# Tile 0's last quarter of features ahead of the last product, and a gate's copy between tile 1's halves, at the end of the second layer's output projection

## What is computed

```python
y = jnp.concatenate([y_sc, y_mla, y_cf, y_na], axis=-1) @ p["w_out"]
x = x + ga1 * rmsnorm(y, p["g_post_mix"])
hm = rmsnorm(x, p["g_pre_mlp"]) * (1 + sc2) + sh2
x = x + ga2 * rmsnorm(sq_relu_mlp(hm, p["w_mlp1"], p["w_mlp2"]), p["g_post_mlp"])
```

## Time and profile before

| | |
|---|---|
| median of three runs | 1489.4 us (1488.3 to 1489.86) |
| the profiled execution's own time | 1490.7 us |
| its span | 1488.8 us |
| TensorE (PE) busy | 1439.2 us, 97% |
| VectorE (DVE) busy | 908.9 us, 61% |
| ScalarE (ACT) busy | 671.6 us, 45% |
| the tail of this change, about | 827 to 851 us of the span |

### The profile page before, as it was taken

The page is one execution under the profiler, slowest core; times in us unless marked ns, Lnnn a source line. Parts: engine busy times, 40 slices in busy tenths (PEclk is TensorE's granted clock), DMA queues, the critical chain, the costliest instruction groups (busy, mean ns, idle before and its releaser), DMA issues.

```text
span 1488.8 us, 23403 instructions
## 1 busy us (share of the span) xinstructions
PE 1439.2 (97%) x9394; PEld 1231.1 (83%) x9394; DVE 908.9 (61%) x1388; ACT 671.6 (45%) x1060; POOL 38.0 (3%) x55
## 2 busy tenths in 40 slices
PE   5999998999999999999999999999999999999998
PEld 3787655888888888889856888998999999798996
DVE  3776555563241433579755665568998545796867
ACT  4421355562140413465155844455444564664544
POOL 0000000000000000000060000000000000000000
PEclk9999999999999999999999999999999999999999
DMA  9421675041331314236375555465445434455553
GB/s 394 160 85 57 236 290 211 4 159 65 114 112 59 132 35 144 82 126 218 114 269 212 198 189 178 147 221 184 170 170 170 165 133 145 142 195 192 176 198 114
DMA packets 33562, 236.95 MB, mean 159 GB/s; under 512 B 3712, under 2 KB 3840, under 8 KB 5696
## 3 DMA queue, kind: packets, MB, share of 16 engines
q1 hardware_dynamic: 32080, 228.31, 42.3%
q0 software_dynamic: 1392, 7.34, 1.5%
HBM read 234.58 MB, written 1.05 MB: 158 GB/s over the span
## 4 chain that ended last, share of the span: by engine, by line
PE 85%; DVE 5%; ACT 4%; DMA 4%; issue 1%; SPq 0%; DVEq 0%; ACTq 0%
PE ps L551 44%; PE ps L597 23%; PE ps L571 4%; DMA w<-in_stream 3%; PE ps L760 2%; PE ps L653 1%; PE ps L840 1%; PE ps L956 1%; DVE w_lo L436 1%; DMA U<-in_start 1%; PE ps L989 1%; PE ps L973 1%; ACT w_hi L426 1%; PE ps L961 1%; PE ps L689 1%
## 5 line engine op out<-in xcount | busy, mean ns | idle before, releaser
L551 PE MATMUL ps<-h_hi,w_hi 128*128 128x256 f32 (+1 forms) x1504 | 468.6, 312 | 3.7 <-DVE h_lo L2487 0.9
L551 PE MATMUL ps<-h_hi,w_lo 128*128 128x256 f32 (+1 forms) x1504 | 464.7, 309 | 0.0
L551 PE MATMUL ps<-h_lo,w_hi 128*128 128x256 f32 (+1 forms) x1504 | 464.6, 309 | 0.0
L426 ACT ACTIVATE w_hi<-w 128x1024 fp32r<-128x1024 f32 x332 | 333.2, 1053 | 246.3 <-DMA w<-in_stream 246.2
L436 DVE TENSOR_TENSOR w_lo<-w,w_hi 128x1024 fp32r<-128x1024 f32 x332 | 390.7, 1219 | 82.1 <-ACT w_hi L426 77.4
L551 PEld LDWEIGHTS ps<-h_hi,w_hi 128*128 128x128 f32 x1504 | 287.0, 191 | 20.6 <-issue 3.2
L551 PEld LDWEIGHTS ps<-h_lo,w_hi 128*128 128x128 f32 x1504 | 287.1, 191 | 15.0 <-issue 0.5
L551 PEld LDWEIGHTS ps<-h_hi,w_lo 128*128 128x128 f32 x1504 | 287.0, 191 | 14.5
L597 PE MATMUL ps<-w_hi,g_hi 128*128 128x512 f32 x472 | 185.0, 392 | 1.7 <-DVE g_lo L2340 0.9
L597 PE MATMUL ps<-w_lo,g_hi 128*128 128x512 f32 x472 | 183.8, 389 | 0.0
L597 PE MATMUL ps<-w_hi,g_lo 128*128 128x512 f32 x472 | 183.8, 389 | 0.0
(11 more groups left out here) (291 smaller groups left out, 1749.6 us busy)
## 6 DMA issues: line engine op xcount, KB each, us to landing
w<-in_stream SPq DMA_DIRECT2D x206, 1024.0 KB, 4.9
U<-in_start SPq DMA_DIRECT2D x4, 1024.0 KB, 11.4
w<-in_start SPq DMA_DIRECT2D x2, 1024.0 KB, 10.8
GA<-in_start SPq DMA_DIRECT2D x2, 1024.0 KB, 14.2
U<-in_bias POOLq DMA_DIRECT2D x2, 1024.0 KB, 6.0
SW<-in_small POOLq DMA_DIRECT2D x2, 896.0 KB, 5.0
X<-in_x SPq DMA_DIRECT2D x1, 1024.0 KB, 5.0
X<-in_ctx SPq DMA_DIRECT2D x1, 1024.0 KB, 7.2
```

Source lines behind the costliest of these rows:

```text
L426: act.activation(k.w_hi[:, c.slot, half], k.w[:, c.slot, half], ACT.Copy).then_inc(k.hi_done, 1)
L551: last = pe.matmul(k.banks(2 * c.pair, n, j * (512 if tiles == 2 else n)), w[a][:, c.slot, at:at + 128], h[b][:, kt * stride:kt * stride + n],
```

## The change

On VectorE, part 3 of tile 0's features (one cast, one subtraction) is done right behind part 2, ahead of `product(1, 1)`, instead of behind `residual(1)`. On ScalarE, the copy of the second half gate stands between parts 0, 1 and parts 2, 3 of tile 1's features, instead of ahead of part 0. Nothing is added or removed, and TensorE's, GpSimd's and SyncE's orders are the same.

```diff
@@ act_tail
     if f.to in ("mlp1", "ffn"):
         turn(0)
-    if f.to == "mlp1":
-        act_mod_step(k, act, LAST_GATES[1], 3)
     if f.row is not None:
         row_features(1)
+    elif f.to == "mlp1":
+        features(1, (0, 1))
+        act_mod_step(k, act, LAST_GATES[1], 3)
+        features(1, (2, 3))
     elif f.to:
         features(f.tiles - 1, range(HF_PARTS))
@@ dve_tail
         elif f.to == "mlp1" and t:
-            features(0, (2,))
+            features(0, (2, 3))
         elif f.to and t:
             features(t - 1, (0,))
         product(t, 1)
@@ dve_tail
         elif f.to:
-            if t:
-                features(t - 1, (3,) if f.to == "mlp1" else (2, 3))
+            if t and f.to != "mlp1":
+                features(t - 1, (2, 3))
             norm(t)
```

## The result

Over 22 runs of each, taken in turn, the changed kernel's median is 1493.49 us (1491.20 to 1495.39) and the kernel before's 1490.34 us (1488.30 to 1496.71). The ratio is 1.0015, interval [1.0008, 1.0021]: +2.2 us, between 1.2 and 3.1. It is slower, by less than the 0.2% that the prediction took as its bound (the interval ends at 0.21%), yet clear of no change, and its median lies above the range that was given.

The account below looks back on a forecast made before the run. TensorE, busy for 97% of the span, was taken as the bound, so only its idle stretches counted. Chain +0.61 and copy +0.43 gave +1.0 us on the median 1489.4: 1490.4 us, range 1488.7 to 1492.0.

Parts of the forecast that it names:

- The moved pair lengthens tile 1's chain: VectorE's moved cast and subtraction delay tile 1's residual, scaling and transposes; its first products start +0.61 us late, range 0.45 to 0.70.
- the other tail: Another tail of the same make: transposes 0.63 us after scaling, features 0.66 later; full clock despite a 1.19 us idle stretch.
- The time that the moved pair takes on VectorE: Cast and subtraction ahead of the product: 0.70 us from the trace, chosen over the skill's 0.90.
- The copy between the halves: ScalarE's copy delays parts 2 and 3, so TensorE waits amid tile 1's 24 products: +0.43 us, ends 0.3 and 0.53.
- The stall ahead of the restart moves with the rest: TensorE's 0.77 us wait for ScalarE's reading L1678, ahead of 850.50, stays and shifts with the chain to 851.5.
- TensorE's clock falls: Rival, chance 0.04: new idle stretches drop TensorE to 1.2 GHz for tile 1's 24 products, +4.0 us in all, 1493.4 us.
- one with a fall: Earlier TensorE wait of 2.3 us for a transfer, at 785 us; a 5 us stretch there shows mean clock 0.84.
- the sum: Chain +0.61 and copy +0.43 give +1.0 us on the whole time, ends +0.75 and +1.25; forecast chance 0.62.
- a fall for half of them: Half clock for half of tile 1's 24 products: +2.5 us, still within 0.2%.
- The copy is hidden: Rival, chance 0.20: no wait amid tile 1's products, only the first term stays, +0.6, 1490.0 us.
- The shift is absorbed: Rival, chance 0.07: a later wait that does not follow TensorE ends last, so the end stays, 1489.4 us.
- the gain is kept: Rival, chance 0.05: tile 1's chain has 0.7 us of room, so the first stall's 0.74 + 0.09 us come off, 1488.6 us.

Follow-up runs that it names:

- e1: Against the kernel before: only VectorE's part of the change, ScalarE's order put back. Ratio 0.9999 [0.9991, 1.0008].
- e4: Kernel before plus one unused cast and subtraction on VectorE ahead of the last product, nothing moved. Ratio 1.0001 [0.9992, 1.0010].
- e2: Kernel before with only ScalarE's part of the change, VectorE's order as before. Ratio 1.0004 [0.9994, 1.0014].
- e7: Whole change plus unused matmuls of 512 and 256 columns ahead of tile 1's transposes and products; against the kernel before, ratio 1.0006 [0.9997, 1.0015].
- e3: Whole change plus one unused 512-column float32 matmul behind the second gate; against the kernel before, ratio 1.0000 [0.9991, 1.0009].
- e8: Kernel before with only ScalarE's sine moved ahead of the second turn. Ratio 0.9993 [0.9984, 1.0002].
- e10: Kernel before with ScalarE's sine moved ahead of the second turn, a second time. Ratio 0.9994 [0.9980, 1.0007].
- e6: Whole change plus one unused cast and subtraction on VectorE ahead of the last product; against the kernel before, ratio 1.0023 [1.0014, 1.0032].
- e11: Kernel before with only the gate's copy moved, behind all of tile 1's features. Ratio 0.9995 [0.9984, 1.0007].
- e5: The whole change, unaltered, once more against the kernel before. Ratio 1.0016 [1.0004, 1.0028].
- e9: VectorE's part of the change alone, a second time, against the kernel before. Ratio 1.0003 [0.9991, 1.0015].
- e12: The whole change, unaltered, a third time against the kernel before. Ratio 1.0000 [0.9989, 1.0012].

## Why the prediction was wrong, point by point

**The moved pair lengthens tile 1's chain: right.** Forecast +0.61, measured +0.53 in the change and alone in e1. Part by part: the product was +0.66 late (forecast 0.70), and the transposes began 0.54 us after the scaling (forecast 0.63, from the other tail), the features 0.70 after them (0.66). With the 0.54, the room that tile 1's chain had before was 838.30 - (837.62 + 0.54) = 0.14 us, not the 0.05 read off the other tail, and 0.66 - 0.14 gives the measured lateness. e4 shows for TensorE's other way to the transposes that VectorE's lateness comes out whole (0.68).

**The time that the moved pair takes on VectorE: the trace was the better guide.** The pair took 0.67 us, from the part 3 cast at 834.47 to the product at 835.14. By the rule of the Trainium skill (page "VectorE: DVE Perf Modes", section "The DRAIN you can't avoid") it would have been 0.90, an estimate. The same section says that a next instruction that is not held starts earlier, and the trace agrees with that.

**The copy between the halves: right in size.** Forecast +0.43, measured +0.41 in e2; both together +1.00 in e7 and +0.97 in e3, against a forecast of 1.04. In the executions with a fall it cost nothing of its own (24.83 without it, 24.66 to 24.87 with it): TensorE shows no wait for the features there, since at half clock it comes to part 2 later.

**The stall ahead of the restart moves with the rest: right.** It is 0.78 us after and 0.77 before, and 0.77 or 0.78 in all other kernels but e8, e10 (none) and e6 (0.60).

**TensorE's clock falls: the step that failed.** The prediction had it as a rival with a chance of 0.04, priced at +3.0 us for all 24 products, and argued from the idle stretches that it lay between a case with no fall (1.19 us) and one with a fall (2.3 us). The mechanism and the place were as that rival said. The step that failed is the sum's taking the clock at nothing: the chance was far too low, and the price was off too.

The chance: the prediction placed the new stretches between its two cases, and gave no reason for so low a number as 0.04. Its case without a fall, the other tail's wait of 1.19 us, was moreover one execution. In e10's profile the clock fell in that tail, which no edit touches, behind the same wait and a second of 0.47 us:

```profile
671.94 1.06 PE L669 MATMUL ps<-C,Y 128*128 128x128 f32 x8 [1.19 <-DVE Y L1906]
673.47 0.35 PE L551 MATMUL ps<-h_hi,w_hi 128*128 128x256 f32 x1 [0.47 <-DVE w_lo L436]
674.00:675.00 1.00, 1.00 (x6) 1.00 (x6) 0.96 (x3) 1.00 (x4) 0.00 (x0) 0.50 1.13 78
```

The other 13 profiles have 1.00 there. In the joint, of five profiles with this pair of stretches, four show the fall; of the six without the new stretch (before, e2, e4, e8, e10, e11) and the two with it filled (e3, e7) none does. The mean clocks point to fewer. Four sets of runs have this pair and the kernel before on the same chip: e1, e5, e9 and e12 are lower by 0.0002, 0.0005, 0.0006 and -0.0001, 0.0003 on average, where 0.0011 would be one fall in each execution. That is an estimate of 0.3 falls in an execution; the scatter of the runs leaves anything from near 0 to 0.5, if falls elsewhere are as frequent in both kernels, which isn't shown. (The 22 runs of the result have 0.9986; the clocks of the kernel before beside them are not on record.) So how often it falls stays open; 0.04 was far under both the four of five and the estimate of 0.3.

The price: where it fell, the joint was 24.66 to 24.87 us, that is +0.86 to +1.07 over the 23.80 without it, since the clock was back after about half of the products. The prediction had named that case, a fall for half of them, at +2.5 in all, 1.5 of it the clock. A fall for all 24 needed e6's longer stretch, and cost 26.39 - 23.83 - 0.68 = 1.9 us over e7 and e4's chain, not 3.0. The wait for the copy (0.43) disappears in it, and a product at half clock is followed by the next after 0.21 us, not after twice the 0.12 us of full clock:

```profile
842.44 0.41 PE L689 MATMUL ps<-w_hi,h_lo 128*128 128x256 f32 x1
842.65 0.41 PE L689 MATMUL ps<-w_hi,h_hi 128*128 128x256 f32 x1
```

In place of +1.0 us the sum should have been +1.0 plus 0.3 to 0.8 of 0.9, +1.3 to +1.7.

**The anchor and the range.** The three runs shown before had a median of 1489.4; 22 runs have 1490.34, and the 35 of the first set of experiments 1491.77. I allowed about 1 us for this, as the three runs lay 1.6 apart. Single runs of the same kernel spread over 8 us. The median after, 1493.49, is 1.5 us above the range's end and 3.1 above the forecast of 1490.4. Of the 3.1, 0.9 is the anchor and 0.3 to 0.7 the clock's part by the sum above. The rest, 1.5 to 1.9 us, no profile places: the two medians lie 3.15 us apart, where the ratio gives +2.2 with an interval from 1.2 to 3.1.

**What the whole program shows of it.** The three sets of the unaltered change give 1.0015, 1.0016 and 1.0000, with 95% intervals of 0.65 to 1.2 parts in a thousand to either side. Weighted by their precision they average about +1.8 us, between +1.1 and +2.6. The joint's +1.9 with a fall lies in that interval, its +1.0 without one just below; a mixture of the two fits, and the average alone doesn't say which. The third set is at the edge: its interval ends at +1.8 us, and that of the first begins at +1.2. The direction of the sum was right, and the ratio is within the bound of 0.2% in all three. But the prediction held differences of up to 3.0 us to be beyond what can be told from none, and 22 runs of each told 2.2 us from none.

**The rivals.** "The copy is hidden" holds in the executions with a fall, for another reason than I gave. "The shift is absorbed" and "the gain is kept" fell: no profile shows either.

## What to carry to other kernels

A stall removed ahead of one group of products is worth nothing if the work that is moved forward lands in the chain to the next group: read the slack of that chain first (here 0.14 us) and compare it with what is put in front of it (0.66 us). When an order gathers TensorE's idle time into fewer, longer stretches close together, reckon with its clock too, look at the granted clock in several executions, and use the mean over all runs beside them, as one profile can miss it; falls elsewhere in the program enter that mean. An unused matmul in such a stretch is a cheap test. As a remedy it brought the mean clock back (0.9993 in e7, against 0.9986 in e5 on the same chip); the time of the whole program points the same way (1.0006 against 1.0016), but the two intervals overlap.

## What the runs showed of the hardware

Idle stretches of 1.35 and 1.03 us, with ten small matmuls between them (eight from 839.50, two from 840.43), let TensorE fall to 1.2 GHz in four profiled executions out of five; the same total with the stretches further apart (1.40 and 1.08 us, with 14 matmuls of products and gate and ten small ones between) did not in the one profile, and the mean clock of 11 runs was that of the kernel before. With 2.02 and 1.03 us the one profile fell for longer, and no run of 11 had a mean clock of 0.999 or more. In e5 the fall came about 0.4 us after the second stretch had ended, with TensorE at work. The Trainium skill (page "TensorE: Matmul & The Clock Gate", section "What's actually happening") says that the default is the throttled state, and that activity releases it. The runs agree in that the clock fell in or just behind idle stretches and came back while products ran (844 to 845 in the profile of the change), and they add that whether stretches of this size are enough differs from one execution to the next. Even 1.19 and 0.47 us were followed by a fall in one profile of 14 (e10, near 675 us). Which feature of an execution decides it was not tried.
